# Local attention in a hybrid decoder layer: the oldest key tile scored in a unit of its own

## The chip, the cores and the metric

The kernel runs on one core of a Trainium2 chip. The metric is the device time of one execution in microseconds, lower is better. A core has five engines with instruction streams of their own: TensorE (PE, with its weight loads PEld), VectorE (DVE), ScalarE (ACT), GpSimd (POOL) and SyncE (SP). They wait for each other by semaphores only, and each runs its stream in order.

## The reference: what is computed

One inference step of a decoder layer with two groups of attention heads. The prompt has 1024 tokens, 8 tiles of 128 queries. The first group has 8 heads of 64 in two key groups `g`, four heads `r` each, and adds three gated branches: attention over compressed keys ("cmp"), over selected blocks ("sel") and over a window of the last 512 keys ("win", the local attention). The second group is latent attention with 4 heads ("mla"). Eight sample rows with caches of 2048 tokens follow, and projections before and after. The window branch, cut to what matters here:

```python
def window_attend(q, q_pos, k, v, k_pos, rel_bias):
    s = einsum('bntgrd,bnsgd->bngrts', q, k) * HD_A ** -0.5
    dist = q_pos[:, :, None] - k_pos[:, None, :]
    bias = rel_bias[rel_bucket(dist)]
    valid = (dist >= 0) & (dist < WINDOW) & (k_pos[:, None, :] >= 0)
    p = masked_softmax(s + bias, valid)
    return einsum('bngrts,bnsgd->bntgrd', p, v)
```

From query tile 4 on, a tile of queries sees five key tiles: its own, the three before it whole, and of the fifth and oldest only the keys that are less than 512 back.

## The kernel before

All data are float32. The program goes through projections, preparation, prompt attention (about 384 to 752 us), the output projection of the prompt, and the decode loop over the sample rows. The change is in prompt attention; all of it is built by the same planner in lines 1516 to 1625 and then issued by one function an engine.

**Units and chunks.** `STAGES` (1516) lists query tile and branch; for tiles 4 to 7 the order is all cmp, then sel, win, mla for each tile. A stage has two halves (two of the four `r` each). `UNITS` (1522 to 1531) holds the pieces of work: for sel and win a unit is one `r` with both key groups, four units a stage; for mla two heads, two units a stage. A unit's scores are the queries against `nb` key tiles. For win from tile 4 on `nb` is 5, and `key_runs` (1645) gives two runs: the four newer key tiles (512 columns) and the oldest one (128 columns). Groups (`GROUPS`, one a half) share an output in PSUM.

**Slots.** Scores lie in PSUM banks 0 to 3, seen as two slots of two banks. A unit with more than four key tiles takes both slots (1544), others alternate. `PREV` says which unit held the slots last and `QK_AT[u]` which units' scores may be issued once unit `u` is the one in work: those whose slots `u` held. `PSLOTS` are the four SBUF buffers for the exponentials, two for a unit with two slots.

**What each engine does in unit u.** `pe_scores` (1659) waits until the exponentials of the unit that held the slots are done (between two units with two slots the first run needs only the first two of four exponentials), then issues the score matmuls (line 1690; for mla 1677 and 1686). VectorE's `extremes` (1824) finds the negated row maximum: a reduction over the columns without a bias (1838 or 1844) and a fused add-and-minimum over those with one (1871). ScalarE's `expo` (1774) takes the exponential of 512-column pieces and what is left, four a unit with more than four key tiles (1787 with a running sum, 1790 without). TensorE turns the probabilities in chunks of up to four tiles (`turns`, 1730, line 1736) into banks 4 and 5 alternately, so the turn of chunk c waits until chunk c-2 has been copied. The copy (`evac`, 1813) is ScalarE's (1806) or VectorE's (1818) by `BY_A` (1573): of a unit's three chunks the first is ScalarE's, the others VectorE's. Two chunks later (`AV_LAG`, 1576) TensorE multiplies with the values: at tile 4 the turned probabilities are the stationary operand (line 1714), from tile 5 on the values are (`crossed`, line 1711) and two chunks are turned before the products of the two before them. In the latter case the group's output is turned back (1742) after ScalarE's copy (`out_copy`, 1795), and `dve_finish` (1890) scales it.

The order on ScalarE matters here (1797 to 1808):

```python
early = lambda v: v < N and len(SLOTS[v]) == 1 and len(SLOTS[v - 1]) == 1
for u in range(N):
    if early(u + 1):
        expo(u + 1)
    for c in CH_OF[u]:
        ...
            evac(act, c, lambda o, i: act.activation(o, i, ACT.Copy), s_evA)
    if u + 1 < N and not early(u + 1):
        expo(u + 1)
```

Before attention, GpSimd copies the window mask into columns 256 to 383 of the bias table `BTX` for all eight heads (1503), and `extremes` adds it to the oldest key tile's scores in the fused operation (384 columns).

Of the kernel before, what the change touches and what calls it, by code (L numbers as in the profile page):

```python
# [17 lines left out]
ALU = mybir.AluOpType  # L18
# [96 lines left out]
def build(nc, x_prompt, x_sample, cache_nsa, cache_mla, state_win, page_table, c_prompt, c_sample,  # L115
# [3 lines left out]
    with ExitStack() as ctx:  # L119
# [137 lines left out]
        NM2 = small(2)  # L257
        NM = small(16).rearrange("p (s g) -> p s g", s=2)
# [1238 lines left out]
        def pool_prep(pool):  # L1497
# [4 lines left out]
            for h in range(H):  # L1502
                pool.tensor_copy(BTX[:, h, 256:384], wmask).then_inc(s_btw, 1)
# [39 lines left out]
        for u, (kind, i, half, heads, k0, nb, og) in enumerate(UNITS):  # L1543
            if nb > 4:
                SLOTS.append((0, 1))
            else:
                SLOTS.append((toggle,))
                toggle = 1 - toggle
# [3 lines left out]
            PSLOTS.append([(turn + n) % 4 for n in range(len(SLOTS[u]))])  # L1552
            PPREV.append([pholds[p] for p in PSLOTS[u]])
            turn += len(SLOTS[u])
            for p in PSLOTS[u]:
                pholds[p] = u
            EX0.append(EX0[u] + len(heads))
        TWO = [len(s) == 2 for s in SLOTS]
        QK0, EXP0 = [0], [0]
        for u in range(N):  # L1560
            QK0.append(QK0[u] + (2 if TWO[u] else 1))
            EXP0.append(EXP0[u] + (4 if TWO[u] else len(UNITS[u][3])))
# [3 lines left out]
        for u, (kind, i, half, heads, k0, nb, og) in enumerate(UNITS):  # L1566
            tiles = 2 if kind == "cmp" else len(heads) * nb
# [5 lines left out]
            BY_A += [k < (1 if n == 3 else (n + 1) // 2) for k in range(n)]  # L1573
# [32 lines left out]
        def exps_for(c):  # L1606
# [6 lines left out]
            if TWO[u]:  # L1613
# [18 lines left out]

        s_alone = sem("s_alone")
# [25 lines left out]
        def pe_scores(pe, u):  # L1659
# [4 lines left out]
            if before >= 0:  # L1664
                pe.wait_ge(s_exp, EXP0[before] + 2 if split else EXP0[before + 1])
# [13 lines left out]
            for m, (o, kb, n) in enumerate(runs):  # L1679
# [3 lines left out]
                for gi, (r, g) in enumerate(heads):  # L1683
# [4 lines left out]
                    else:  # L1688
                        keys = KSELT if kind == "sel" else KWINT
                        mm = pe.matmul(scores(u, gi, o, o + P * n), QT[rg, r, q], keys[rg, ks], start=True, stop=True)  # L1690
# [79 lines left out]
        def act_attention(act):  # L1770
# [3 lines left out]
            def expo(u):  # L1774
                kind, i, half, heads, k0, nb, og = UNITS[u]
                n = 64 if kind == "cmp" else P * nb
                parts = [(gi, lo, min(n, lo + 512)) for lo in range(0, n, 512) for gi in range(len(heads))]
                for gi, lo, hi in parts:
                    o = head_at(u, gi)
                    act.wait_ge(s_neg, EX0[u] + (len(heads) if kind == "cmp" else gi + 1))  # L1780
                    if room_for(u, gi):
                        act.wait_ge(s_trc, room_for(u, gi))
                    if crossed(u):
                        slot = 2 * (heads[gi][0] % 2) + heads[gi][1] + (4 if lo else 0)
# [1236 lines left out]
```

## Time and profile before

| | |
|---|---|
| median of 3 runs | 1117.63 us (1115.32 to 1119.17) |
| the profiled execution's own time | 1116.44 us |
| its span | 1114.3 us |
| TensorE busy | 1074.0 us, 96% |
| VectorE busy | 618.8 us, 56% |
| ScalarE busy | 359.9 us, 32% |
| GpSimd busy | 88.9 us, 8% |
| score matmuls of sel and win (L1690) | 384, 75.0 us |
| turns of probabilities (L1736) | 704, 112.2 us |
| products with the values (L1714; L1711 is its crossed form) | 768, 99.6 us |

The profiled execution is one run with the hardware profiler on; its span is the time from its first to its last instruction. Matmuls are pipelined, so the busy time of TensorE takes in the time in which one matmul's end overlaps the next one's beginning. The start times of neighbouring rows of the timeline are the safer measure of what a piece of work costs.

### The profile page before, as it was taken

The numbers are of one execution on the slowest core, as the hardware profiler recorded it, in microseconds if no ns is written. First come the engines' busy times: TensorE is split into PE (matmuls) and PEld (weight loads), VectorE is DVE, ScalarE is ACT, GpSimd is POOL, SyncE is SP. The second block draws the span as 40 slices with busy tenths as digits, with TensorE's granted clock in tenths as the row PEclk, the third lists the DMA queues.
The fourth block names the chain that finished last, engine by engine and source line by source line (L and its number), as shares of the span: only waits on it lengthen the run. The fifth ranks groups of instructions, "written<-read, shape, count | busy, mean of one in ns | idle before, by whom it ended". The sixth has DMA issues, their size and how long they took to land.

```text
span 1114.3 us, 22552 instructions
## 1 busy us (share of the span) xinstructions
PE 1074.0 (96%) x8364; PEld 768.0 (69%) x8364; DVE 618.8 (56%) x1613; ACT 359.9 (32%) x875; POOL 88.9 (8%) x192
## 2 busy tenths in 40 slices
PE   6899999999999999998999999999999999999997
PEld 2455599998886687777876766764545476777775
DVE  0635323463423477767676666742324588888883
ACT  0422001121112475545455555631112123333330
POOL 0210100110000111100101010011000200000000
PEclk8999999999999999999999999999999999999997
DMA  9933260011006230000000000005794367788881
GB/s 350 314 114 95 79 204 2 16 35 56 1 1 123 55 106 1 1 1 1 2 1 2 1 1 1 1 1 120 162 316 150 135 220 267 268 273 290 276 216 57
DMA packets 96612, 120.25 MB, mean 108 GB/s; under 512 B 31569, under 2 KB 65380, under 8 KB 95480
## 3 DMA queue, kind: packets, MB, share of 16 engines
q1 hardware_dynamic: 96504, 118.81, 34.5%
q8 instruction: 68, 1.11, 0.4%
q14 instruction: 40, 0.33, 0.1%
HBM read 104.41 MB, written 14.36 MB: 107 GB/s over the span
## 4 chain that ended last, share of the span: by engine, by line
PE 84%; issue 8%; SPq 3%; DVE 3%; ACT 1%; DMA 1%; POOL 0%; ACTq 0%; POOLq 0%; DVEq 0%
PE PS L548 19%; PE PS L2047 10%; PE PS L1736 7%; PE PS L1714 7%; PE PS L1690 6%; PE PS L540 4%; PE PS L2549 3%; PE PS L1677 3%; PE PS L1711 3%; PE PS L2511 2%; PE PS L2562 2%; PE PS L1686 2%; PE PS L1242 1%; PE PS L647 1%; SPq L376 1%
## 5 line engine op out<-in xcount | busy, mean ns | idle before, releaser
L548 PE MATMUL PS<-AR 128*128 128x256 f32 (+2 forms) x896 | 219.7, 403 | 0.0
L548 PEld LDWEIGHTS PS<-AR 128*128 128x128 f32 x896 | 167.8, 190 | 45.2 <-issue 6.2
L1736 PE MATMUL PS<-CA,AR 128*128 128x128 f32 x704 | 112.2, 282 | 0.2 <-ACT AR L1790 0.2
L2047 PE MATMUL PS<-AR 128*128 128x512 f32 x256 | 112.3, 592 | 0.0
L962 DVE TENSOR_TENSOR AR<-PS,AR 128x256 f32<-128x256 f32 (+2 forms) x80 | 36.2, 453 | 134.0 <-PE PS L548 133.9
L1806 ACT ACTIVATE AR<-PS 128x512 f32<-128x512 f32 (+1 forms) x108 | 58.2, 546 | 138.6 <-PE PS L1736 137.9
L1736 PEld LDWEIGHTS PS<-CA,AR 128*128 128x128 f32 x704 | 77.9, 144 | 34.9 <-issue 25.8
L1714 PE MATMUL PS<-AR 128*128 128x65 f32 (+1 forms) x768 | 99.6, 270 | 0.0
L1714 PEld LDWEIGHTS PS<-AR 128*128 128x128 f32 x768 | 94.2, 192 | 0.2
L1790 ACT ACTIVATE AR<-PS,SM_ 128x512 f32<-128x512 f32 (+4 forms) x208 | 83.6, 475 | 17.8 <-DVE SM_ L1871 10.2
L2047 PEld LDWEIGHTS PS<-AR 128*128 128x128 f32 x256 | 47.5, 190 | 54.0 <-issue 54.0
L1690 PE MATMUL PS<-AR 64*128 64x512 f32 (+3 forms) x384 | 75.0, 496 | 6.0 <-ACT AR L1790 4.1
L1838 DVE TENSOR_REDUCE SM_<-PS 128x1 f32<-128x512 f32 (+2 forms) x80 | 42.0, 566 | 62.3 <-PE PS L1686 31.8
L1818 DVE COPY AR<-PS 128x512 f32<-128x512 f32 (+1 forms) x100 | 56.9, 585 | 9.8 <-PE PS L1736 8.8
L1787 ACT ACTIVATE AR<-PS,SM_ 128x512 f32<-128x512 f32 (+3 forms) x96 | 54.3, 582 | 2.6 <-DVE SM_ L1871 1.9
L759 ACT ACTIVATE AR<-PS 128x256 f32<-128x256 f32 (+2 forms) x20 | 8.0, 402 | 139.2 <-PE PS L548 98.1
L1690 PEld LDWEIGHTS PS<-AR 64*128 64x128 f32 x384 | 31.7, 187 | 30.8 <-ACT AR L1787 11.5
L2140 DVE TENSOR_TENSOR AR<-PS,AR 128x512 f32<-128x512 f32 x16 | 11.1, 692 | 71.0 <-PE PS L2047 71.0
L540 PE MATMUL PS<-AR 128*64 128x128 f32 x896 | 49.8, 273 | 0.0
L540 PEld LDWEIGHTS PS<-AR 128*64 128x64 f32 x896 | 48.8, 137 | 1.3 <-issue 1.2
L1949 POOL TENSOR_TENSOR AR<-AR 128x256 f32<-128x256 f32 x32 | 23.2, 726 | 328.8 <-DVE AR L1937 328.2
L1871 DVE CUSTOM_DVE_ANT_0 PS<-PS,AR,SM_ 128x256 f32<-128x256 f32 (+1 forms) x96 | 47.4, 535 | 1.7
(360 smaller groups left out, 1574.3 us busy)
## 6 DMA issues: line engine op xcount, KB each, us to landing
AR<-in_cache_nsa SPq DMA_DIRECT2D x128, 256.0 KB, 4.7
AR<-in_cache_mla SPq DMA_DIRECT2D x128, 96.0 KB, 3.6
AR<-in_x_prompt SPq DMA_DIRECT2D x16, 512.0 KB, 4.6
AR<-in_w_ada SPq DMA_DIRECT2D x3, 2048.0 KB, 11.8
AR<-in_w_in SPq DMA_DIRECT2D x6, 1024.0 KB, 8.7
AR<-in_w_ada SPq DMA_DIRECT2D x8, 512.0 KB, 4.4
AR<-in_w_out SPq DMA_DIRECT2D x4, 1024.0 KB, 11.4
AR<-in_w_out SPq DMA_DIRECT2D x2, 2048.0 KB, 17.5
```

The source lines that it names most:

```text
L540: mm = pe.matmul(bank[64 * h:64 * h + 64, P * r:P * r + P], weights[:, k, h, 64 * r:64 * r + 64], tokens[:, k, :], start=(fresh and r == 0 ...
L548: mm = pe.matmul(bank[:, 0:WIDE[g]], tokens[:, k, :], w, start=(fresh and k == 0), stop=(last and k == 3), skip_group_check=True)
L1690: mm = pe.matmul(scores(u, gi, o, o + P * n), QT[rg, r, q], keys[rg, ks], start=True, stop=True)
L1714: mm = pe.matmul(out, tile, v, start=(n == 0), stop=(n == nb - 1))
L1736: mm = pe.transpose(PS[:, 4 + c % 2, P * (t - t0):P * (t - t0) + P], tile(u, t), ident)
L1787: act.activation(probs(u, gi, lo, hi), PSF[:, o + lo:o + hi], ACT.Exp, bias=NM[:, u % 2, gi:gi + 1], scale=-1.0, accum_out=TOT[og % 4][:, ...
L1790: act.activation(probs(u, gi, lo, hi), PSF[:, o + lo:o + hi], ACT.Exp, bias=NM[:, u % 2, gi:gi + 1], scale=-1.0).then_inc(s_exp, 1)
L1806: evac(act, c, lambda o, i: act.activation(o, i, ACT.Copy), s_evA)
L1818: copy(PTB[:, c % 4, 0:nt, :], PS[:, 4 + c % 2, 0:P * nt].rearrange("p (t q) -> p t q", t=nt)).then_inc(done, 1)
L1838: dve.tensor_reduce(nm[:, gi:gi + 1], scores(u, gi, 0, min(far, 512)), AX, ALU.min) .then_inc(s_mx, 1)
L1871: dve.tensor_tensor_reduce(s, s, bias, 1.0, nm[:, gi:gi + 1] if far else 1e29, ALU.add, ALU.min, nm[:, gi:gi + 1]).then_inc(s_neg, 1)
L2047: mm = pe.matmul(PS[0:n, 2 + 2 * (m % 2) + c, :], YTO[m % 2][:, f, 0:n], weights[:, f, 512 * c:512 * c + 512], start=(f == 0), stop=(f == 7))
```

## The change

- A new unit of kind "old" stands before the win units of each half from query tile 4 on (8 in all). It holds the scores of all four heads of the half against the oldest key tile, in one slot, and has no exponentials, no chunks and no probability buffer.
- A win unit from tile 4 on takes one slot instead of two and scores only the four newer key tiles. It still has five tiles of probabilities, four exponentials and three chunks.
- VectorE adds the mask to the old unit's scores into the bias table's columns 256 to 383 (in SBUF), and reduces them to a minimum for each head in the new `EM`. `extremes` of a win unit takes the minimum with `EM` in a short extra operation, and its fused operation covers 256 columns instead of 384.
- The exponentials of the fifth tile read those kept scores from SBUF instead of PSUM.
- The third chunk of such a unit is copied by ScalarE instead of VectorE.
- `early` is a question of the slots of two units that follow each other without the old ones, so it is now true between the win units of a stage.
- GpSimd's eight mask copies go, and two waits with them.

```diff
@@ units and slots
             for half in range(2):
+                if kind == "win" and i >= 4:
+                    UNITS.append(("old", i, half, [(r, g) for r in (2 * half, 2 * half + 1) for g in range(G)], k0, 1, len(GROUPS)))
@@
-            if nb > 4:
+            if nb > 4 and kind != "win":
                 SLOTS.append((0, 1))
@@
-            PSLOTS.append([(turn + n) % 4 for n in range(len(SLOTS[u]))])
+            PSLOTS.append([(turn + n) % 4 for n in range(0 if kind == "old" else 2 if nb > 4 else 1)])
@@
-            EX0.append(EX0[u] + len(heads))
+            EX0.append(EX0[u] + (0 if kind == "old" else len(heads)))
         TWO = [len(s) == 2 for s in SLOTS]
+        MANY = [unit[5] > 4 for unit in UNITS]
+        OLD = [unit[0] == "old" for unit in UNITS]
+        WHOLE = [u for u in range(N) if not OLD[u]]
+        NTH = [sum(not old for old in OLD[:u]) for u in range(N)]
@@
-            BY_A += [k < (1 if n == 3 else (n + 1) // 2) for k in range(n)]
+            BY_A += [k != 1 if kind == "win" and n == 3 else k < (1 if n == 3 else (n + 1) // 2) for k in range(n)]
@@ head_at
+            if OLD[u]:
+                return 1024 * SLOTS[u][0] + 512 * (gi % 2) + P * (gi // 2)
@@ key_runs
-                return [(0, k0 + 1, 4), (512, k0, 1)]
+                return [(0, k0 + 1, 4)]
@@ pe_scores
-            if before >= 0:
-                pe.wait_ge(s_exp, EXP0[before] + 2 if split else EXP0[before + 1])
+            if before >= 0 and OLD[before]:
+                pe.wait_ge(s_old, sum(OLD[:before + 1]))
+            elif before >= 0:
+                pe.wait_ge(s_exp, EXP0[before] + 2 if split or MANY[before] and not TWO[before] else EXP0[before + 1])
@@ expo
+                    sc = BTX[:, R * g + r, 256:384] if kind == "win" and lo else PSF[:, o + lo:o + hi]
-                        act.activation(probs(u, gi, lo, hi), PSF[:, o + lo:o + hi], ACT.Exp, bias=NM[:, u % 2, gi:gi + 1],
+                        act.activation(probs(u, gi, lo, hi), sc, ACT.Exp, bias=NM[:, at, gi:gi + 1],
@@ act_attention
-            early = lambda v: v < N and len(SLOTS[v]) == 1 and len(SLOTS[v - 1]) == 1
+            early = lambda u, v: len(SLOTS[v]) == 1 and len(SLOTS[u]) == 1
             expo(0)
-            for u in range(N):
-                if early(u + 1):
-                    expo(u + 1)
+            for u, v in zip(WHOLE, WHOLE[1:] + [None]):
+                if v is not None and early(u, v):
+                    expo(v)
@@ dve_attention
+            def oldest(u):
+                _, i, half, heads, k0, nb, og = UNITS[u]
+                dve.wait_ge(s_qk, QK0[u + 1])
+                past = [v for v in WHOLE if UNITS[v][0] == "win" and UNITS[v][1:3] == (i - 1, half)] if i > 4 else []
+                if past:
+                    dve.wait_ge(s_exp, EXP0[past[-1] + 1])
+                kept = BTX[:, :, 256:384].rearrange("p (g r) c -> p g r c", g=G)[:, :, 2 * half:2 * half + 2, :]
+                dve.tensor_tensor(kept, scores(u, 0, 0, 1024).rearrange("p (g r c) -> p g r c", g=G, c=P)[:, :, 0:2, :],
+                                  wmask.rearrange("p (g r c) -> p g r c", g=1, r=1).to_broadcast([P, G, 2, P]), ALU.add)\
+                    .then_inc(s_old, 1)
+                dve.wait_ge(s_old, sum(OLD[:u + 1]))
+                dve.tensor_reduce(EM[:, 4 * half:4 * half + 4].rearrange("p (r g) -> p g r", g=G), kept, AX, ALU.min)\
+                    .then_inc(s_mx, 1)
@@ extremes
-                near = {"cmp": 64, "mla": P, "sel": min(256, P * nb),
-                        "win": min(256, P * nb) if i < 4 else 384}[kind]
-                far = 0 if kind == "cmp" else P * nb - near
+                kept = kind == "win" and i >= 4
+                near = {"cmp": 64, "mla": P, "sel": min(256, P * nb), "win": min(256, P * nb)}[kind]
+                far = 0 if kind == "cmp" else P * (nb - kept) - near
@@
+                    if kept:
+                        r2 = heads[0][0] % 2
+                        dve.tensor_tensor(nm, nm, EM[:, 4 * half + 2 * r2:4 * half + 2 * r2 + 2], ALU.min).then_inc(s_mx, 1)
@@ pool_prep
-            for h in range(H):
-                pool.tensor_copy(BTX[:, h, 256:384], wmask).then_inc(s_btw, 1)
```

Elsewhere the tests for two slots become tests for more than four tiles (`MANY`) where probabilities are meant, and the double buffer of the negated maxima goes by `NTH` instead of the unit's number.

## Rows read from the trace of the kernel before

**Rows 1.** The page, busy time of TensorE, its share and instructions.
```profile
PE 1074.0 (96%) x8364; PEld 768.0 (69%) x8364; DVE 618.8 (56%) x1613; ACT 359.9 (32%) x875; POOL 88.9 (8%) x192
```

**Rows 2.** Busy by stretch (length, PE, PEld, DVE, ACT, POOL), local stages, tiles 4, 5.
```profile
524.80:552.40 27.60, 27.60 (x230) 23.69 (x229) 20.17 (x58) 14.27 (x30) 1.45 (x2) 1.00 0.01 2
583.00:605.20 22.20, 20.89 (x201) 14.21 (x198) 16.60 (x50) 14.09 (x45) 1.45 (x2) 1.00 0.01 1
```

**Rows 3.** Timeline (start us, us, what), TensorE, local units of tile 5.
```profile
595.02 0.44 PE L1742 MATMUL PS<-CA,AR 128*128 128x128 f32 x2
...
595.95 1.35 PE L1690 MATMUL PS<-AR 64*128 64x512 f32 x8 [0.49 <-ACT AR L1787]
...
597.23 1.09 PE L1736 MATMUL PS<-CA,AR 128*128 128x128 f32 x8
...
598.25 0.88 PE L1711 MATMUL PS<-AR 128*64 128x128 f32 x12
...
599.06 0.44 PE L1736 MATMUL PS<-CA,AR 128*128 128x128 f32 x2
...
600.13 1.35 PE L1690 MATMUL PS<-AR 64*128 64x512 f32 x8
```

**Rows 4.** Timeline of the same stretch, ScalarE and VectorE.
```profile
597.92 0.60 ACT L1806 ACTIVATE AR<-PS 128x512 f32<-128x512 f32 x1 [1.33 <-PE PS L1736]
...
598.63 0.69 ACT L1787 ACTIVATE AR<-PS,SM_ 128x512 f32<-128x512 f32 x1
...
600.31 0.37 ACT L1787 ACTIVATE AR<-PS,SM_ 128x128 f32<-128x128 f32 x1
...
601.31 0.76 DVE L1838 TENSOR_REDUCE SM_<-PS 128x1 f32<-128x256 f32 x2 [1.30 <-PE PS L1690]
```

**Rows 5.** Prices: groups by form (busy, mean ns), and timeline of tiles 3 and 0.
```profile
L1844 DVE TENSOR_REDUCE SM_<-PS 128x2 f32<-128x512 f32 x6 | 4.1, 683 | 0.0
...
L1871 DVE CUSTOM_DVE_ANT_0 PS<-PS,AR,SM_ 128x256 f32<-128x256 f32 x32 | 14.4, 491 | 0.6
...
476.55 1.13 PE L1690 MATMUL PS<-AR 64*128 64x512 f32 x4
477.61 0.66 PE L1736 MATMUL PS<-CA,AR 128*128 128x128 f32 x4
...
384.39 0.71 PE L1690 MATMUL PS<-AR 64*128 64x128 f32 x8
```

**Rows 6.** Timeline, last selected unit into the first local one, tiles 5, 6.
```profile
586.17 1.40 PE L1690 MATMUL PS<-AR 64*128 64x512 f32 x8 [0.28 <-ACT AR L1787]
...
586.45 0.49 ACT L1787 ACTIVATE AR<-PS,SM_ 128x256 f32<-128x256 f32 x1
...
644.04 0.60 ACT L1787 ACTIVATE AR<-PS,SM_ 128x384 f32<-128x384 f32 x1
...
644.12 1.35 PE L1690 MATMUL PS<-AR 64*128 64x512 f32 x8
```

**Rows 7.** Timeline, first latent unit behind the local ones, tiles 4 and 5.
```profile
555.98 0.65 PE L1736 MATMUL PS<-CA,AR 128*128 128x128 f32 x4
...
557.66 1.78 ACT L1790 ACTIVATE AR<-PS,SM_ 128x512 f32<-128x512 f32 x4 [0.38 <-DVE SM_ L1871]
...
558.15 0.39 PE L1736 MATMUL PS<-CA,AR 128*128 128x128 f32 x2
...
559.22 2.04 PE L1677 MATMUL PS<-AR 128*128 128x512 f32 x5
...
611.23 0.44 PE L1736 MATMUL PS<-CA,AR 128*128 128x128 f32 x2
...
611.39 1.99 ACT L1790 ACTIVATE AR<-PS,SM_ 128x512 f32<-128x512 f32 x4 [0.70 <-DVE SM_ L1871]
```

**Rows 8.** Timeline, and busy by stretch with granted clock behind POOL's (1.00 is full).
```profile
518.78 2.32 PE L1690 MATMUL PS<-AR 64*128 64x512 f32 x8 [1.97 <-ACT AR L1790]
...
519.00:522.40 3.40, 3.40 (x15) 2.17 (x14) 1.65 (x5) 0.47 (x2) 0.00 (x0) 0.50 0.02 5
```

More of the change, by code:

```diff
@@ L257, in build @@
         NM2 = small(2)
+        EM = small(8)
         NM = small(16).rearrange("p (s g) -> p s g", s=2)
@@ L1551, in build @@
                 holds[s] = u
[L1552 removed]
+            PSLOTS.append([(turn + n) % 4 for n in range(0 if kind == "old" else 2 if nb > 4 else 1)])
             PPREV.append([pholds[p] for p in PSLOTS[u]])
[L1554 removed]
+            turn += len(PSLOTS[u])
             for p in PSLOTS[u]:
                 pholds[p] = u
[L1557 removed]
+            EX0.append(EX0[u] + (0 if kind == "old" else len(heads)))
         TWO = [len(s) == 2 for s in SLOTS]
+        MANY = [unit[5] > 4 for unit in UNITS]
+        OLD = [unit[0] == "old" for unit in UNITS]
+        WHOLE = [u for u in range(N) if not OLD[u]]
+        NTH = [sum(not old for old in OLD[:u]) for u in range(N)]
         QK0, EXP0 = [0], [0]
@@ L1566, in build @@
         for u, (kind, i, half, heads, k0, nb, og) in enumerate(UNITS):
-            tiles = 2 if kind == "cmp" else len(heads) * nb
+            tiles = 2 if kind == "cmp" else 0 if kind == "old" else len(heads) * nb
             CH_OF.append([])
@@ L1689, in pe_scores @@
                         keys = KSELT if kind == "sel" else KWINT
-                        mm = pe.matmul(scores(u, gi, o, o + P * n), QT[rg, r, q], keys[rg, ks], start=True, stop=True)
+                        mm = pe.matmul(scores(u, gi, o, o + P * n), QT[64 * g:64 * g + 64, r, q], keys[64 * g:64 * g + 64, ks],
+                                       start=True, stop=True)
                 if TWO[u] or m == len(runs) - 1:
@@ L1806, in act_attention @@
                         evac(act, c, lambda o, i: act.activation(o, i, ACT.Copy), s_evA)
-                if u + 1 < N and not early(u + 1):
-                    expo(u + 1)
+                if v is not None and not early(u, v):
+                    expo(v)
             for c in range(NCH, NCH + AV_LAG + 2):
@@ L1822, in dve_attention @@
             far_count = [0]
+            def oldest(u):
[11 more added lines that the diff above has]
+                    .then_inc(s_mx, 1)
+                far_count[0] += 1
             def extremes(u):
+                if OLD[u]:
+                    return oldest(u)
                 kind, i, half, heads, k0, nb, og = UNITS[u]
                 dve.wait_ge(s_qk, QK0[u] + 1)
-                if u >= 2:
-                    dve.wait_ge(s_exp, EXP0[u - 1])
-                nm = NM[:, u % 2, 0:len(heads)]
-                near = {"cmp": 64, "mla": P, "sel": min(256, P * nb),
-                        "win": min(256, P * nb) if i < 4 else 384}[kind]
-                far = 0 if kind == "cmp" else P * nb - near
+                if NTH[u] >= 2:
+                    dve.wait_ge(s_exp, EXP0[WHOLE[NTH[u] - 1]])
+                nm = NM[:, NTH[u] % 2, 0:len(heads)]
+                kept = kind == "win" and i >= 4
+                near = {"cmp": 64, "mla": P, "sel": min(256, P * nb), "win": min(256, P * nb)}[kind]
+                far = 0 if kind == "cmp" else P * (nb - kept) - near
                 if far:
@@ L1865, in extremes @@
                     return
-                if kind == "win" and i == 4:
-                    dve.wait_ge(s_btw, 8)
                 for gi, (r, g) in enumerate(heads):
@@ L1876, in dve_attention @@
             for u in range(N):
-                for og in FIN_AT[CH_OF[u][0]]:
+                for og in FIN_AT[CH_OF[u][0]] if CH_OF[u] else []:
                     dve_finish(dve, og)
@@ L1917, in dve_finish @@
             else:
-                if TURNS_BACK[og] and TWO[last]:
+                if TURNS_BACK[og] and MANY[last]:
                     dve.tensor_tensor(TOT[og % 4][:, 0:4], TOT[og % 4][:, 0:4], TOT[og % 4][:, 4:8], ALU.add).then_inc(s_cl, 1)
-                    dve.wait_ge(s_cl, 2 + sum(TURNS_BACK[o] and TWO[GROUPS[o][3]] for o in range(og + 1)))
+                    dve.wait_ge(s_cl, 2 + sum(TURNS_BACK[o] and MANY[GROUPS[o][3]] for o in range(og + 1)))
                 dve.reciprocal(RC, o[:, :, 64] if not TURNS_BACK[og] else TOT[og % 4][:, 0:4]).then_inc(s_rc, 1)
```

16 lines of the change are left out of this document (10 added, 6 removed).

## The prediction

> **What bounds the kernel now.** I read the page first: TensorE is busy 96% of the span [rows 1], so the matrix engine sets the time and another engine matters only where TensorE waits for it. Then busy time by stretch, over the local-attention stages of query tiles 4 and 5 [rows 2]: at tile 4 TensorE is busy for all of 27.60 us; at tile 5 for 20.89 of 22.20, and tiles 6 and 7 look like tile 5. Then the timeline of one local-attention unit of tile 5 [rows 3, 4]. There are four such units W0 to W3 a tile. TensorE does the scores of the next unit, turns chunks a and b (four probability tiles each) of this one, multiplies the last two chunks of the previous unit with the values, turns chunk c (two tiles), multiplies a. Every other unit it also turns an output back, and there the next scores start 0.93 us after that pair of turns, 0.56 later than the 0.37 that the pair takes, since ScalarE's exponentials came behind its copy of the output. So what can be won is small: 0.56 at W2, as much at the MLA unit behind W3, which shows the same pattern, and a few hundredths beside them. That is 1.2 us of the 1.31 that TensorE idles at tile 5 [rows 2], 3.7 for tiles 5 to 7, nothing at tile 4.
>
> **What the change does to the order.** The oldest key tile gets a unit of its own a half (8 in all), and the local units fit in one slot of scores instead of two. Two consequences of the code decide the case.
>
> First, the scores still run only one unit ahead. Slots alternate old, W0, W1, old, W2, W3; the scores of W1 are issued in the turn of the first "old" and those of W2 in the turn of W1, both just before W0's and W1's probabilities are turned. The old units take the place that a second unit ahead would have.
>
> Second, "early" now holds between neighbouring local units. ScalarE issues the four exponentials of the next unit before its copy of chunk a. Before, it copied a first (597.92 ahead of 598.63 [rows 4]). Chunk c's turn needs a's bank, so TensorE, which waits for no ScalarE copy now, will wait behind exponentials whose maxima VectorE has not yet found.
>
> **The new wait, from s = start of the next unit's scores.** TensorE: a 512-column visit takes 1.06 us to the following turn (476.55 to 477.61 [rows 5]); turning a and b 1.02 (597.23 to 598.25 [rows 3]); values 0.81 (to 599.06). It wants to turn c at s+2.89. The other side: the scores are complete and VectorE starts at s+1.18 (600.13 to 601.31 [rows 3, 4]); one reduction of 512 columns 0.68 [rows 5]; the small minimum against the kept one about 0.2 (an estimate: two short instructions); the first fused add-and-minimum 0.49 [rows 5] and 0.1 until ScalarE begins: s+2.67. Four exponentials hold ScalarE for 2.0 us (598.63 to 600.31, and 0.36 for the last [rows 4]): s+4.67. The copy takes 0.60 [rows 4] and TensorE sees it at s+5.33. The wait is 2.44 us at W1 and at W2. At W0 the second old unit's scores (0.6) and sometimes one more pair of value products fill part of it: 1.7. W3 is followed by a two-slot unit, so it has no early exponentials and no such wait. Tiles 5 to 7: 3 x (1.7 + 2.44 + 2.44) = **19.7 us**. At tile 4 the four exponentials take 1.78 [rows 7], so the copy is seen near s+5.03; turns and values interleave there, and c comes 2.17 after a (555.98 to 558.15 [rows 7]), at s+3.23: waits of 1.2, 1.8, 1.8, **4.8 us**.
>
> **The other parts.** *Old units on TensorE.* The fifth key run costs 0.22 a visit today (1.28, from 595.95 to 597.23 [rows 3], less 1.06), four times a tile. An old unit is eight 64x128 instructions; the nearest row, the same eight at tile 0, took 0.71 with its tail of about 0.2 [rows 5]. Between 0.44 and 0.71 I take 0.6, twice a tile: +0.3 a tile, **+1.2** (0 to +2.2).
> *Entry.* Both first score groups now wait for all four exponentials of the last selected unit, where two were enough. At tile 5 the last ends at 586.94 and the scores began at 586.17; at tile 6, 644.64 against 644.12 [rows 6]. With 0.1 to react: 0.9, 0.6, as much at tile 7, 0.1 at tile 4: **+2.2**.
> *Copy of chunk c to ScalarE.* At W0 to W2 it is short and lies in what is counted. At W3 it stands before the exponentials of the first MLA unit. Tile 4: c is turned from 558.15, is ready about 0.45 later and takes 0.39, so the exponentials start near 559.0, not 557.66; two of them take 1.25 (0.57 to the second and its own 0.68, of four in 1.78) and the second MLA scores start near 560.35, not 559.22 [rows 7]: +1.1. Tile 5: turned from 611.23, exponentials at 612.1 instead of 611.39 [rows 7]: +0.7, and the same at 6 and 7. **+3.2**.
> *Removed waits*: **-3.7**, as above.
> *VectorE.* Two reductions of 256 and two fused operations of 384 columns become one of 512, a small minimum and two of 256, and each old unit adds an addition and a reduction of 512 elements, nearest the 0.68 row, so 1.4 a half. It has been busy 16.6 of 22.2 us [rows 2] and the stage gets longer; cover is there, at W0 too, whose exponentials I find done before the second old scores want the slot. 0; if the cover were gone, 0.7 a half, 5.6 us in all, on the slow side.
> *Reading kept scores.* The 32 narrow exponentials read the kept scores from SBUF. I take them at their price now. The Trainium skill (Perfetto Trace Analysis, Optimizing Scalar/DVE Operations) gives ScalarE about 42 ns more per access from SBUF than from PSUM; by that the twelve waits would grow by 0.08 each and the sum by 1.0, and no row here shows it.
> *GpSimd* loses eight copies of the mask ahead of attention; TensorE's start there hangs on its own work, and I cost this at 0.
>
> **The clock.** Its one fall in attention: TensorE idle 1.97 us before 518.78, then 3.40 us at a granted 0.50, which is 1.2 GHz [rows 8]. A stretch of 3.4 us at half rate costs at most 1.7. The six waits of 2.44 at tiles 5 to 7 are this long, but the work between them is denser than it was around 518. Bounds: no fall, 0; six, +10. I take two, **+3**. The Trainium skill (TensorE: Matmul & The Clock Gate, What's actually happening) says that the default is the throttled state and activity releases it, which speaks against this change: by it alone all six could fall.
>
> **Sum.** 19.7 + 4.8 + 1.2 + 2.2 + 3.2 - 3.7 + 3 = +30.4 on the profiled execution's 1116.44, which lies 1.2 under the median of the runs: 1147.
>
> **Rivals.** *Every long wait drops the clock*, or VectorE's cover is gone as well: 1154 to 1160. For it: row 518.78. Against: the dense work between. Chance 0.2. *The waits are half as long*, because VectorE reaches the maxima sooner or exponentials start in the gaps of the previous unit: 12 us less, no falls: about 1131. Chance 0.14. *No new wait at all*: the maxima are there before the copy is due. It decides whether the first early exponential starts by s+0.2; then entry, old units, MLA and removed waits leave +2.9, 1119. Chance 0.06; against it stands that VectorE cannot begin before s+1.18. *Faster*: the same, and the entry and MLA delays are hidden behind TensorE's own queue too, so that only the removed waits count: -3.7, 1113. It would need scores two units ahead as in tiles 0 to 3. Chance 0.05.
>
> **The numbers.** The forecast has a chance of 0.55, the two slower or milder neighbours 0.2 and 0.14. The range goes from the halved waits, 1130, to the clock case, 1160. A measurement of this kernel can tell about 0.3%, 3.4 us, from no change: faster 0.05, same 0.06, slower 0.89.
>
> **What would show it.** In the new timeline: at tiles 5 to 7, 6.3 to 6.7 us from scores to scores at W1 and W2 instead of 4.2 (595.95 to 600.13 [rows 3]); turn instructions of chunk c idle by some 2.4 us, released by ScalarE's copy; that copy directly behind four exponentials; the three waits of 0.49 before scores gone; the first MLA exponentials after a 256-column ScalarE copy. I am wrong if the copy of a comes before the exponentials, if TensorE is still busy over 90% in these stages, or if it waits for VectorE's additions instead.

## The result, and the profile after

The changed kernel takes 1155.89 us (median of 4 runs, 1151.18 to 1156.82) beside 1116.47 for the kernel before (4 runs, 1112.96 to 1119.17): a ratio of 1.0346 [1.0304, 1.0389], 39.4 us slower. The profiled execution took 1156.82, 1.9 more than its span. The first lines of its page answer to [rows 1]:

```profile
span 1154.9 us, 22566 instructions
PE 1094.4 (95%) x8364; PEld 780.4 (68%) x8364; DVE 620.1 (54%) x1613; ACT 365.5 (32%) x891; POOL 86.5 (7%) x184
```

TensorE issues as many matmuls as before, so its work has not grown; its busy time has, by 20.4 us, and its idle time by 20.2. Both have to be explained. I split the span at two marks that both timelines show: the first score matmul of attention and the first turn of the output projection.

| | before | after |
|---|---|---|
| up to attention | 384.39 | 384.35 |
| attention | 369.94 | 410.45 |
| from there to the end | 359.96 | 360.05 |

All of the loss is in attention. Busy time by stretch for the local stages of tiles 4 to 7 (length, PE, PEld, DVE, ACT, POOL, granted clock; 1.00 is full), the first two answering to [rows 2]:

```profile
537.10:561.60 24.50, 20.55 (x153) 16.37 (x153) 14.38 (x41) 10.57 (x23) 2.90 (x4) 0.93 0.00 1
599.00:626.60 27.60, 22.14 (x167) 14.10 (x168) 13.66 (x37) 12.58 (x41) 1.37 (x2) 0.81 0.00 1
666.70:694.70 28.00, 22.40 (x168) 14.40 (x169) 13.78 (x38) 13.07 (x42) 1.44 (x2) 0.82 0.00 1
739.40:766.70 27.30, 21.48 (x179) 14.39 (x180) 14.31 (x38) 13.07 (x42) 1.44 (x2) 0.87 0.00 1
```

At tile 5 TensorE is idle 5.5 us of the stage where it was idle 1.3 [rows 2], and its clock is at 0.81 where it was at 1.00. The stretches are cut by eye; measured from W0's first scores to the first latent unit's scores, the stages of tiles 4 to 7 took 18.35, 18.96, 19.12 and 19.77 us before and take 24.47, 27.63, 28.02 and 27.26 now.

The timeline from W0's turn in work to W1's at tile 5, TensorE and ScalarE with VectorE's reduction and fused operation, answers to [rows 3, 4] (start, us, what; in brackets the idle time before it and who ended it):

```profile
603.68 1.57 PE L1700 MATMUL PS<-AR 64*128 64x512 f32 x12
...
604.86 0.69 DVE L1870 TENSOR_REDUCE SM_<-PS 128x2 f32<-128x512 f32 x1 [0.80 <-PE PS L1700]
605.18 1.09 PE L1747 MATMUL PS<-CA,AR 128*128 128x128 f32 x8
605.58 0.16 DVE L1881 TENSOR_TENSOR SM_<-SM_ 128x2 f32<-128x2 f32 x1
605.78 0.49 DVE L1904 CUSTOM_DVE_ANT_0 PS<-PS,AR,SM_ 128x256 f32<-128x256 f32 x1
...
606.37 0.69 ACT L1801 ACTIVATE AR<-PS,SM_ 128x512 f32<-128x512 f32 x1 [1.62 <-DVE SM_ L1904]
...
607.04 0.68 ACT L1801 ACTIVATE AR<-PS,SM_ 128x512 f32<-128x512 f32 x1
...
607.70 0.40 ACT L1801 ACTIVATE AR<-AR,SM_ 128x128 f32<-128x128 f32 x1
...
608.09 0.39 ACT L1801 ACTIVATE AR<-AR,SM_ 128x128 f32<-128x128 f32 x1
...
608.47 0.58 ACT L1819 ACTIVATE AR<-PS 128x512 f32<-128x512 f32 x1
...
609.20 0.41 PE L1747 MATMUL PS<-CA,AR 128*128 128x128 f32 x2 [1.90 <-ACT AR L1819]
...
610.79 2.08 PE L1700 MATMUL PS<-AR 64*128 64x512 f32 x4
...
612.80 1.38 PE L1747 MATMUL PS<-CA,AR 128*128 128x128 f32 x8
...
614.42 0.69 ACT L1801 ACTIVATE AR<-PS,SM_ 128x512 f32<-128x512 f32 x1 [4.39 <-DVE SM_ L1904]
...
616.53 0.58 ACT L1819 ACTIVATE AR<-PS 128x512 f32<-128x512 f32 x1
...
617.26 0.66 PE L1747 MATMUL PS<-CA,AR 128*128 128x128 f32 x2 [2.27 <-ACT AR L1819]
```

Chunk a is turned from 605.18 and could be copied from about 605.8 (chunk b's half of the same eight turns comes behind it). ScalarE stands until 606.37 at an exponential whose maximum VectorE is still finding, does all four, and copies a (L1819) from 608.47. TensorE has multiplied what it had and waits 1.90 us to turn chunk c into a's bank. At W1 the same wait is 2.27, at W2 1.29:

```profile
625.38 0.41 PE L1747 MATMUL PS<-CA,AR 128*128 128x128 f32 x2 [1.29 <-ACT AR L1819]
```

The view of waits adds up one such wait in each of W0 to W2 of the four tiles (us in total, number, longest):

```profile
PE PS L1747 <- ACT AR L1819: 20.8, 12, 2.6
```

The clock is the second part. The same four score matmuls take 2.08 us from 610.79 and took 1.13 at tile 3 [rows 5]. Stretches of TensorE at its lower level, with the granted clock behind POOL's column:

```profile
548.60:552.00 3.40, 3.40 (x14) 1.91 (x12) 1.71 (x6) 0.27 (x1) 0.00 (x0) 0.50 0.00 0
...
610.00:613.40 3.40, 3.40 (x13) 1.40 (x10) 1.41 (x5) 0.03 (x1) 0.72 (x1) 0.50 0.00 0
616.90:623.60 6.70, 6.34 (x30) 3.88 (x32) 2.49 (x7) 1.66 (x5) 0.00 (x0) 0.50 0.00 0
...
388.20:398.40 10.20, 10.20 (x50) 8.95 (x50) 4.76 (x26) 4.65 (x16) 0.00 (x0) 0.50 1.02 295
```

0.50 is 1.2 GHz. Within or right behind the local stages there are seven of them at tiles 4 to 7 (548.6, 562.2, 610.0, 616.9, 678.3, 685.1, 756.8), four of 3.4 us and three of twice that, so ten times 3.4. The last line is different: it lies at tile 0, in code that the change leaves alone, and the profile of before does not have it. On the other hand, before has 3.4 us at 0.50 from 519.0 [rows 8], ahead of the local stages, and the changed kernel has none there.

### The profile page after: what moved, and what is told of

Its sections match the earlier page's. It is cut to its first block, busy times and chain, and to the rows that moved or that the text cites. A ratio compares the mean times of both kernels' runs of the same rounds, so it can differ in the third digit from the quotient of the medians.

```text
span 1154.9 us, 22566 instructions
## 1 busy us (share of the span) xinstructions
PE 1094.4 (95%) x8364; PEld 780.4 (68%) x8364; DVE 620.1 (54%) x1613; ACT 365.5 (32%) x891; POOL 86.5 (7%) x184
## 4 chain that ended last, share of the span: by engine, by line
PE 82%; issue 8%; ACT 3%; SPq 3%; DVE 3%; DMA 1%; POOL 0%; ACTq 0%; POOLq 0%; DVEq 0%
PE PS L549 19%; PE PS L2080 10%; PE PS L1747 8%; PE PS L1725 7%; PE PS L1700 7%; PE PS L541 4%; PE PS L1687 3%; PE PS L2582 3%; PE PS L1722 3%; PE PS L2544 2%; PE PS L2595 2%; PE PS L1696 2%; ACT AR L1801 1%; PE PS L1243 1%; PE PS L648 1%
## 5 line engine op out<-in xcount | busy, mean ns | idle before, releaser
L1747 PE MATMUL PS<-CA,AR 128*128 128x128 f32 x704 | 117.3, 292 | 21.0 <-ACT AR L1819 20.8
L1747 PEld LDWEIGHTS PS<-CA,AR 128*128 128x128 f32 x704 | 81.3, 149 | 68.8 <-issue 38.2
L1819 ACT ACTIVATE AR<-PS 128x512 f32<-128x512 f32 (+1 forms) x124 | 64.1, 524 | 139.5 <-PE PS L1747 138.6
L1725 PE MATMUL PS<-AR 128*128 128x65 f32 (+1 forms) x768 | 102.1, 275 | 0.6 <-DVE AR L1970 0.6
L1700 PE MATMUL PS<-AR 64*128 64x512 f32 (+3 forms) x384 | 80.7, 528 | 6.5 <-ACT AR L1804 4.1
L1868 DVE TENSOR_REDUCE SM_<-PS 128x1 f32<-128x512 f32 (+1 forms) x48 | 29.9, 664 | 52.9 <-PE PS L1696 37.4
L1801 ACT ACTIVATE AR<-PS,SM_ 128x512 f32<-128x512 f32 (+2 forms) x72 | 46.0, 650 | 34.2 <-DVE SM_ L1904 33.9
L1831 DVE COPY AR<-PS 128x512 f32<-128x512 f32 (+1 forms) x84 | 51.1, 617 | 8.9 <-PE PS L1747 8.2
L2173 DVE TENSOR_TENSOR AR<-PS,AR 128x512 f32<-128x512 f32 x16 | 11.1, 692 | 71.0 <-PE PS L2080 71.0
L1870 DVE TENSOR_REDUCE SM_<-PS 128x2 f32<-128x512 f32 (+2 forms) x38 | 24.0, 633 | 45.5 <-PE PS L1700 33.5
```

The costliest lines, as they stand in the source:

```text
L1700: mm = pe.matmul(scores(u, gi, o, o + P * n), QT[64 * g:64 * g + 64, r, q], keys[64 * g:64 * g + 64, ks], start=True, stop=True)
L1725: mm = pe.matmul(out, tile, v, start=(n == 0), stop=(n == nb - 1))
L1747: mm = pe.transpose(PS[:, 4 + c % 2, P * (t - t0):P * (t - t0) + P], tile(u, t), ident)
L1801: act.activation(probs(u, gi, lo, hi), sc, ACT.Exp, bias=NM[:, at, gi:gi + 1], scale=-1.0, accum_out=TOT[og % 4][:, slot:slot + 1]).then_i ...
L1831: copy(PTB[:, c % 4, 0:nt, :], PS[:, 4 + c % 2, 0:P * nt].rearrange("p (t q) -> p t q", t=nt)).then_inc(done, 1)
```

## The experiments

Each ratio is to runs of the kernel before on the same chip, with its 95% interval. "Attention" is the second row of the table above, 369.94 before and 410.45 after. A "visit" is the time from one unit's first score matmul to the next unit's. Of the ten ranges that I gave, those of 5, 7 and 9 held; the time of 8 lies 0.6 us above its range, and those of 1, 2, 3, 4, 6 and 10 lie 1.4 to 5.7 us below theirs.

**1. Only the order on ScalarE undone.** The changed kernel, with no early exponentials between two local units:

```diff
-            early = lambda u, v: len(SLOTS[v]) == 1 and len(SLOTS[u]) == 1
+            early = lambda u, v: len(SLOTS[v]) == 1 and len(SLOTS[u]) == 1 and not (MANY[u] and MANY[v])
```

> The changed kernel, but ScalarE issues the exponentials of the next local unit after all its copies of this one, as before the change. Theory (the copy of chunk a waits behind the early exponentials): the twelve long waits before chunk c's turn (20.8 us by the changed kernel's profile) go; in their place the scores of W2 and of the first latent unit wait about 1.2 us a time for exponentials that now stand behind the copy of chunk c, some 2.7 us a tile. That is 13 to 15 us less, and the clock falls behind the long waits go as well, about 10: 1128 to 1136 us. Rival (the maxima come late whatever ScalarE's order is, since scores run one unit ahead): the same waits turn up before the turn of chunk a, and the time stays within 5 us of the changed kernel's 1156.

1122.32 us, 1.0059 [1.0033, 1.0085]; attention 379.52. One condition takes 33.6 of 39.4 us away, and no stretch of half rate is left in the local stages. The exponentials now come behind chunk c's copy too, and the next scores wait for them. From the timeline and the waits of this kernel:

```profile
599.13 0.38 ACT L1819 ACTIVATE AR<-PS 128x256 f32<-128x256 f32 x1
599.41 0.68 ACT L1801 ACTIVATE AR<-PS,SM_ 128x512 f32<-128x512 f32 x1
...
600.90 1.13 PE L1700 MATMUL PS<-AR 64*128 64x512 f32 x4 [0.85 <-ACT AR L1801]
```

This is the wait that I expected in place of the first, but smaller than I had costed it: 0.85 us at W2's scores and as much at the first latent unit, not about 1.2. So the time lies 5.7 us under the range that I gave.

**2. Chunk a's copy ahead of the exponentials, c's behind them.**

```diff
-                if v is not None and early(u, v):
+                between = v is not None and early(u, v) and MANY[u] and MANY[v]
+                if v is not None and early(u, v) and not between:
                     expo(v)
                 for c in CH_OF[u]:
...
+                    if between and c == CH_OF[u][-1]:
+                        expo(v)
```

> The changed kernel, but between two local units ScalarE's order is: copy of chunk a, copy of the output where one is due, exponentials of the next unit, copy of chunk c. Theory: no wait before chunk c's turn, exponentials early enough that the next scores wait 0.2 to 0.6 us as before the change, chunk c's copy done before it is needed. What stays of the change is entry +2.2, old units +1.2, the late exponentials of the first latent unit +2 to +3: 1120 to 1126 us. Rival (chunk c's copy behind the exponentials stalls the next unit's chunk b instead): 1135 to 1145 us.

1118.59 us, 1.0017 [0.9997, 1.0038]; attention 373.90, no low stretch in it. All but 2 us of the loss is gone: it was not the old units, nor VectorE, nor the copy of c on ScalarE as such, but one copy behind four exponentials. The timeline has the copy of a 0.9 us ahead of the exponentials and TensorE turning c without a wait, and the scores later as before the change:

```profile
596.55 0.38 ACT L1808 ACTIVATE AR<-PS 128x256 f32<-128x256 f32 x1 [0.88 <-PE PS L1722]
596.83 0.68 ACT L1801 ACTIVATE AR<-PS,SM_ 128x512 f32<-128x512 f32 x1
...
598.33 1.13 PE L1700 MATMUL PS<-AR 64*128 64x512 f32 x4 [0.49 <-ACT AR L1801]
...
600.08 0.60 ACT L1822 ACTIVATE AR<-PS 128x512 f32<-128x512 f32 x1 [0.77 <-PE PS L1747]
...
601.01 0.69 ACT L1801 ACTIVATE AR<-PS,SM_ 128x512 f32<-128x512 f32 x1 [0.33 <-DVE SM_ L1907]
601.21 0.44 PE L1747 MATMUL PS<-CA,AR 128*128 128x128 f32 x2
```

The first three of these lines matter for the forecast: the idle 0.49 before the scores, which I had booked as removed, is there again at its old size. This order puts the copy of the output (L1808) ahead of the exponentials again, as before the change; in the changed kernel the exponentials come first. So the order that gave these waits back is the one that made the long ones.

**3. Chunk c's copy back on VectorE, the order left.**

```diff
-            BY_A += [k != 1 if kind == "win" and n == 3 else k < (1 if n == 3 else (n + 1) // 2) for k in range(n)]
+            BY_A += [k < (1 if n == 3 else (n + 1) // 2) for k in range(n)]
```

> The changed kernel with chunk c's copy given back to VectorE, the early exponentials kept. Theory: the waits before chunk c's turn stay, since they are for the copy of a; only the delay of the first latent unit's exponentials goes (3.2 us forecast, less by the trace at tiles 5 to 7, more at tile 4 where the clock was low): 3 to 6 us less, 1150 to 1153 us. Rival (ScalarE is simply overloaded, the copy of c being what makes it late): 10 to 20 us less, 1136 to 1146 us.

1146.53 us, 1.0271 [1.0243, 1.0299]; attention 403.51. The twelve waits stay and are no shorter:

```profile
PE PS L1747 <- ACT AR L1819: 23.7, 12, 2.6
```

So who copies c is not the cause. The time came out 3.5 us below my range, at the upper edge of the rival's (1136 to 1146), although the mechanism held. The two profiles differ by 10.9 us. Of these, 3.1 come from low stretches ahead of the local stages (none at attention's start here, but one at 519.7 that the changed kernel's profile lacks) and 4.7 lie behind attention (355.36 against 360.05), in code that is the same, again by low stretches. These are differences that a single profile has by chance. The first latent units of tiles 6 and 7, on which no low stretch lies in either profile, are 0.5 us shorter each, as expected. So c's copy is worth a few microseconds at most.

**4. TensorE kept at work through the waits.** Eight turns of tiles that are turned anyway, once more into the same place, ahead of chunk b's turn and so before chunk c's wait, at W0 to W2 (no result uses them twice):

```diff
+                if UNITS[u][0] == "win" and MANY[u] and c == CH_OF[u][1] and UNITS[u + 1][0] != "mla":
+                    for t in range(8):
+                        pe.matmul(PS[:, 4 + c % 2, P * (t % 4):P * (t % 4) + P], tile(u, t0 + t % 4), ident, start=True, stop=True)
```

> The changed kernel with eight extra 128x128 matmuls (sixteen instructions, 1.75 us at the full rate) before the turn of chunk b in W0, W1 and W2 of tiles 4 to 7; they write what the turn then writes again, so the result is the same. They fill the wait before chunk c's turn, which is 1.6 to 2.4 us long, and add no more than a few tenths to the chain. Theory (about 10 us of the loss is TensorE at 1.2 GHz after long waits): the low stretches in tiles 4 to 7 go and the kernel gets 7 to 11 us faster, 1145 to 1149 us, though it does more work. Rival (the low level costs little, since it falls on waits): the same time or up to 4 us more, 1156 to 1160 us.

1142.54 us, 1.0239 [1.0199, 1.0279]; attention 402.31. 96 needless matmuls (8 at each of 12 places) make the changed kernel 13 us faster. In its profile the local stages and the first latent units behind them are 9.4 us shorter, within the 7 to 11 expected; all of attention is 8.1 shorter, and the rest lies ahead of it and behind it, where I count nothing for the same reason as above. Its stretches for tiles 4 and 5:

```profile
537.40:561.50 24.10, 24.10 (x201) 20.94 (x201) 14.37 (x40) 10.59 (x23) 1.45 (x2) 1.00 0.00 1
597.20:621.90 24.70, 23.03 (x215) 17.17 (x215) 13.91 (x37) 12.71 (x41) 1.39 (x2) 1.00 0.01 2
```

The granted clock is 1.00 in both, and there is no half rate left in the local stages of any tile. TensorE still waits for the copy (5.0 us in all, the rest of the waits is filled), and the visits are as long as the copy makes them: at tile 5 they take 4.73, 6.82, 6.45 and 6.73 us. The last two are W1's and W2's, and they bear out the 6.3 to 6.7 of the prediction, which was made for full rate. In the changed kernel the same four are 4.73, 7.11, 8.11 and 7.67.

**5. Both undone: order and copier.** The edits of 1 and 3 together.

> The changed kernel with both orders undone: the exponentials of the next local unit behind ScalarE's copies, and chunk c's copy on VectorE. What is left of the change is the old units, one slot for a local unit, and the wait for all four exponentials at the entry. Theory: the long waits and the delay of the first latent unit are gone; entry costs 2.2 us and the old units next to nothing, since they fill waits: 1115 to 1120 us. Rival (the old units and VectorE's extra operations have a price of their own): 1122 us or more.

1116.01 us, 1.0003 [0.9979, 1.0027]. What is left of the change (old units, one slot, the short minimum, kept scores read from SBUF) neither costs nor brings anything that can be measured. Its interval allows 2 to 3 us either way. Its stages of tiles 5 to 7 take 18.79, 19.01 and 19.67 us, 0.1 to 0.2 less than before, though the entry of tile 5 stays 0.9 us longer.

**6. Chunk c's copy on ScalarE in the kernel before, alone.** The change to `BY_A` put into the kernel before.

> The kernel before, with only chunk c's copy of the local units from tile 4 on moved to ScalarE. There the exponentials of the next unit stand behind all copies, so they start after chunk c is turned and copied. Theory: exponentials come about 1.2 us later at two of four units a tile, 0.4 at the two with an output copy, 0.5 to 1 at the first latent unit: 12 to 16 us slower than before, 1128 to 1133 us. Rival (ScalarE has room, a copy of 0.39 us costs nothing): within 3 us of before, 1114 to 1120 us.

1126.54 us, 1.0086 [1.0055, 1.0117]; attention 381.01, 11.1 longer. Here the exponentials of a local unit are never early, so the copy of c delays them and with them the next scores. Its timeline:

```profile
604.34 0.44 PE L1736 MATMUL PS<-CA,AR 128*128 128x128 f32 x2
...
604.82 0.38 ACT L1806 ACTIVATE AR<-PS 128x256 f32<-128x256 f32 x1 [1.02 <-PE PS L1736]
605.10 0.68 ACT L1787 ACTIVATE AR<-PS,SM_ 128x512 f32<-128x512 f32 x1
...
606.59 1.35 PE L1690 MATMUL PS<-AR 64*128 64x512 f32 x8 [1.22 <-ACT AR L1787]
```

I expected all four units of a tile to be hit; at tile 5 it adds 0.36, 1.18 and 0.36 to three of them, and 0.58 at the latent unit. It shows that an edit can cost 10 us in one order and, as 2 shows, about 2 us or less in another.

**7. Scores two units ahead.** Both old units at the head of the stage, so that the slots that were "old, W0, W1, old" put one unit more between a unit's scores and its turn:

```diff
-                if kind == "win" and i >= 4:
-                    UNITS.append(("old", i, half, [(r, g) for r in (2 * half, 2 * half + 1) for g in range(G)], k0, 1, len(GROUPS)))
+                if kind == "win" and i >= 4 and half == 0:
+                    for hh in range(2):
+                        UNITS.append(("old", i, hh, [(r, g) for r in (2 * hh, 2 * hh + 1) for g in range(G)], k0, 1, len(GROUPS) + hh))
```

> The changed kernel, ScalarE's early order kept, but both old units of a tile stand before its four local units, so that from W0 on the scores run two units ahead. Theory (the early exponentials hurt because the maxima of a unit scored one ahead come too late): waits before chunk c's turn shrink to under 0.6 us; a wait of about 1.9 us for the first exponentials comes once a tile, where the pipeline fills: 1124 to 1134 us. Rival (the early order costs by itself, whatever the scores' lead): 1145 us or more.

1131.97 us, 1.0128 [1.0084, 1.0172]. The order on ScalarE is that of the change, yet 18 of 20.8 us of waits for the copy are gone:

```profile
PE PS L1701 <- ACT AR L1802: 9.0, 6, 2.2
...
PE PS L1748 <- ACT AR L1820: 2.7, 4, 0.7
```

This confirms the first of the prediction's two consequences: early exponentials hurt only because the scores are one unit ahead and the maxima not yet there. The price is in the first line, waits before scores: 2.4 of its 9.0 us are the entries, as in the changed kernel; the other 6.6 are three waits of 2.2 at tiles 5 to 7, where the pipeline is filled again at the head of the stage (at tile 4 the same wait, for L1805, is 2.0). Three of these four are followed by 3.4 us at 0.50 (545.5, 603.5, 733.2), the one at 665.81 is not. Both ways to mend it work on one wait; the copy's place is the cheaper.

**8. The order of 2, and the two later mends.** The last unit's chunk c goes back to VectorE, so that the first latent exponentials come earlier, and the first old unit waits for three exponentials of the last selected unit, not four.

```diff
-            BY_A += [k != 1 if kind == "win" and n == 3 else k < (1 if n == 3 else (n + 1) // 2) for k in range(n)]
+            BY_A += [k != 1 if kind == "win" and n == 3 and (half, heads[0][0]) != (1, R - 1) else k < (1 if n == 3 else (n + 1) // 2) for k in range(n)]
...
-                pe.wait_ge(s_exp, EXP0[before] + 2 if split or MANY[before] and not TWO[before] else EXP0[before + 1])
+                pe.wait_ge(s_exp, EXP0[before] + 3 if OLD[u] and TWO[before] else
+                           EXP0[before] + 2 if split or MANY[before] and not TWO[before] else EXP0[before + 1])
```

> The order of e2_copy_first, with chunk c's copy of the last local unit of a tile (ahead of the first latent unit) given back to VectorE, and the old unit at the entry waiting for three exponentials instead of four. Theory: against e2 the late exponentials of the latent unit (0.96, 0.58, 0.54, 0.49 us by its profile) and about 0.5 us a tile at the entry go, 4 us in all: 1113 to 1117 us, within 0.3% of before on either side. Rival (the gain is taken back by the next wait, for the second latent unit's exponentials): 1117 to 1120 us.

1117.58 us, 1.0007 [0.9986, 1.0027]; attention 370.52, 3.4 less than in 2 although it has one low stretch (520.6, 0.6 us) that 2 has not: the two mends are worth the 4 us in attention that I expected of them. The medians show only 1.0 of it, with intervals that overlap, so the time as a whole lies in the rival's range although the rival's new wait is not there. That the first old unit waits for only two exponentials, as before the change, was not tried.

**9 and 10. The output's copy and turn one chunk later.** What both kernels still have is the idle 0.49 before the scores, where the copy of the output stands ahead of the exponentials. The same edit, on 8 and on the kernel before:

```diff
-... CH_OF[g[3]][-1] + AV_LAG + 1 == c]
+... CH_OF[g[3]][-1] + AV_LAG + 2 == c]
-... CH_OF[g[3]][-1] + AV_LAG + (2 if TURNS_BACK[og] else 1) == c]
+... CH_OF[g[3]][-1] + AV_LAG + (3 if TURNS_BACK[og] else 1) == c]
```

> e8_mended with ScalarE's copy of a finished output, TensorE's turn of it and VectorE's scaling each one chunk later. What is left of TensorE's waits in the local stages of e8 is 0.6 us at the scores of W2 and of the first latent unit, where the output's copy stands before the exponentials. Theory: one chunk later it lies in ScalarE's idle time, those waits and 0.3 at the entry go, some 3 to 4 us in all: 1112 to 1116 us. Rival (the later output holds up its bank or VectorE instead): 1116 us or more.

> The kernel before with the same shift by one chunk and nothing of the change. If the shift is what gains, and not the old units, it gives as much here: the waits of 0.56 us at W2 and the first latent unit and 0.34 at the entry of tile 5 go, 3 to 4 us: 1112 to 1116 us. Rival (only one-slot units can use it): 1116 to 1118 us.

On 8: 1114.22 us, 0.9977 [0.9954, 1.0000]. On the kernel before, with nothing of the change: **1110.57 us, 0.9949 [0.9930, 0.9968]**, the one version that clearly beats both kernels. In its trace the waits of local and latent scores for L1787 are gone from the list, and the stages of tiles 5 to 7 take 18.08, 17.90 and 18.43 us, 3.4 less than before in all; their entries are another 1.0 shorter. The medians differ by 6.2, more than this and more than the 3 to 4 expected; the rest is not explained. From its timeline, copy, exponentials, the turn back and scores:

```profile
600.11 0.39 ACT L1795 ACTIVATE AR<-PS 128x256 f32<-128x256 f32 x1
...
602.38 0.69 ACT L1787 ACTIVATE AR<-PS,SM_ 128x512 f32<-128x512 f32 x1
602.58 0.44 PE L1742 MATMUL PS<-CA,AR 128*128 128x128 f32 x2
...
604.27 0.70 PE L1690 MATMUL PS<-AR 64*128 64x512 f32 x2
```

The copy now lies 2.3 us ahead of the exponentials and no longer delays them. The 3.7 us of removed waits that the change was booked with were to be had by this, without old units.

## Why the prediction was right, and where its size was off

The direction and the mechanism were right: 1155.89 lies within the range of 1130 to 1160, and experiments 1 and 2 remove the named wait by the order on ScalarE, 7 by the lead of the scores. The forecast of +30.4 was 9 us under the 39.4 measured, and the measured time lies among the 1154 to 1160 of the slower rival. By its terms, with the profiles' visits; at full rate means with experiment 4's visits in place of those that hold a low stretch, so the split between clock and the rest is an estimate from two profiles:

| term | forecast | measured |
|---|---|---|
| local stages at full rate: waits, old units, removed waits | 24.5 + 1.2 - 3.7 = 22.0 | 5.4 + 5.8 + 6.0 + 5.8 = 23.1 |
| entry | 2.2 | 0.0 + 0.9 + 0.7 + 0.7 = 2.3 |
| first latent unit at full rate | 3.2 | 1.0 + 0.5 + 0.4 + 0.4 = 2.3 |
| clock | 3 | 2.3 + 2.9 + 2.9 + 1.7 = 9.7 |
| not foreseen: low stretches ahead of the local stages | | 4.1 - 1.0 = 3.1 |
| sum | 30.4 | 40.5 |

Where four values stand they are those of tiles 4 to 7, rounded one by one.

**The new waits** were right in place and number: twelve, none at W3, and those of tile 4 shorter. In size they were right at full rate, a little low: with experiment 5's visits, which have no such wait, beside those at full rate, W0 to W2 of tile 5 come to 1.9, 2.6 and 2.4 us for the 1.7, 2.44 and 2.44 booked, and the twelve to 26.4 for 24.5. In the trace they read 20.8, since work slowed to half rate fills a part of some waits (W2's at tile 5 reads 1.29). The chain behind them held step by step: from W1's scores at 603.68, VectorE starts 1.18 us later, the exponentials 2.69 (2.67 booked), and the copy is seen at 5.52 (5.33 booked). At W1 the exponentials began 3.63 us after the scores (610.79 to 614.42), not 2.67, and this is the clock again: at half rate the scores take 2.0 us to the following turn instead of 1.06, so VectorE starts later too. A low stretch thus costs twice, on TensorE's own work and by a later start of the wait's chain.

**The clock** is the term that was mis-sized: "I take two, +3", where the stages have ten times 3.4 us at half rate, for 9.7 us. I took two stretches at 1.5 each; there were ten at 1.0 each on average. Of the twelve waits seven have a low stretch right behind them or from their last few tenths on: W0's at tiles 4, 5 and 6, W1's at 5, 6 and 7, W2's at 4. I had written that the dense work between the waits spoke against it; that argument had no row behind it, while the one row that there was (idle 1.97, then 3.4 us at 0.50 [rows 8]) spoke for it. The upper bound of 10, for a fall at each of six waits at 1.7, met the sum by luck: the falls were seven, of other lengths and partly at other waits. The rival "every long wait drops the clock", at 0.2, was the better forecast for this term; its other half, VectorE's cover gone, did not occur (VectorE is busy 13.7 of 27.6 us at tile 5). The Trainium skill (TensorE: Matmul & The Clock Gate, What's actually happening) has the throttled state as the default which activity lifts. By that rule a fall could follow every one of the six waits that it was applied to, W1's and W2's of tiles 5 to 7; the trace goes half of that way, with a fall at W1's three. Experiment 4 shows the cause rather than the coincidence: with matmuls in the same waits, the clock of these stages is at 1.00 throughout.

**Removed waits**, -3.7, were there, at 3.0: the six idle times of 0.49 or 0.50 before the scores of W2 and of the first latent unit at tiles 5 to 7 are gone in the changed kernel (at tile 5 the first two exponentials end by 607.72, and the scores start at 610.79) and stand again in experiments 2 and 5. But they went by the same order that made the long waits, so they were no gain that could be kept. **Old units** came to -0.4 instead of +1.2: in experiment 5 the visits with old scores are some 0.2 longer than before and later visits 0.2 to 0.3 shorter. So the first row is 26.4 - 3.0 - 0.4 where 24.5 + 1.2 - 3.7 was booked; its errors nearly cancel, which is luck.

**Entry** came out as worked out. **The latent term** was right at tile 4 (1.0 for 1.1) and over at the others (0.4 for 0.7). **VectorE** and **GpSimd** at nothing were right: experiment 5 has both, and its ratio is 1.0003 [0.9979, 1.0027].

**Kept scores from SBUF.** The narrow exponentials of tiles 5 to 7, read from SBUF in the changed kernel (first line) and from PSUM before (second; busy us, mean ns):

```profile
L1801 ACT ACTIVATE AR<-AR,SM_ 128x128 f32<-128x128 f32 x24 | 9.3, 394 | 0.0
...
L1787 ACT ACTIVATE AR<-PS,SM_ 128x128 f32<-128x128 f32 x24 | 8.7, 376 | 0.0
```

The difference is 18 ns. The Trainium skill (Perfetto Trace Analysis, Optimizing Scalar/DVE Operations) gives about 42 ns more for SBUF; the trace agrees in sign and shows less than half of it. With two such exponentials in each of twelve waits that is 0.4 us, not the 1.0 by the page and not the nothing that I took.

**Ahead of the local stages.** The low stretch of 10.2 us at tile 0 costs 4.1 us: so much later does tile 4's selected stage begin, counted from the start of attention. Of the twelve profiles of this study five have it, among them experiment 10's, whose kernel has nothing of the change. It is no effect of the change, and what sets it is open. The changed kernel's profile gets 1.0 us back, since there the clock does not fall at the place of [rows 8], behind the same idle time:

```profile
522.84 1.35 PE L1700 MATMUL PS<-AR 64*128 64x512 f32 x8 [1.97 <-ACT AR L1804]
```

The medians of several runs hold such chances in part only, so the 39.4 between them may hold a share that the table does not split.

## What to carry to other kernels

Before an engine's work is issued "early", ask what short work of the same engine it will now stand in front of, and when its own inputs are there: four exponentials ahead of one 0.58 us copy cost twelve waits of some 2 us. On an engine that bounds the kernel, price an idle gap of about 2 us with the half rate that follows it (up to 1.7 us for each 3.4, here 1.0 on average) whenever the trace shows one such pair. And when an order is to take small waits away, ask whether they stay away once the waits that the same order makes are mended.

## What the runs showed of the hardware that I had not expected

- Needless work can win time: 96 extra matmuls in the waits, and the kernel went from 1155.89 to 1142.54 us, with the granted clock in the stages of tiles 4 and 5 back from 0.93 and 0.81 to 1.00.
- Idle time of 1.3 to 2.6 us amid dense matmuls was followed by 3.4 us at 0.50 or twice that at seven of twelve waits. Why the other five (0.9 to 1.9 us) passed is open, and length alone does not tell: 1.90 us was followed by a fall at W0 of tile 5 and not at W0 of tile 7, and the same 1.97 us in the same code at the start of tile 4's selected stage in nine of the twelve profiles and not in three. At tile 5 the first ended at 609.20 and the low stretch began at 610.0; the second at 617.26 was already under way when it began at 616.9.
- Code that no edit touched differs between profiles by whole low stretches: at tile 0 none or about 10.2 us of it, for instance in experiment 5, whose line for the same place is below, and from the end of attention to the end of the kernel 355.4 to 360.1 us. A difference of 3 to 5 us in one profile of this kernel is therefore no evidence of an edit.

```profile
388.30:398.50 10.20, 10.20 (x52) 9.05 (x49) 5.00 (x25) 4.36 (x15) 0.00 (x0) 0.50 1.02 295
```
